# Where the last modulation groups of a three-layer transformer are computed: between output units, or in the waits of three normalisations

## The reference, cut to what matters

```python
def adaln(cond, w, b):                      # w: (1024, 6144)
    m = jax.nn.silu(cond) @ w + b
    return [m[:, None, i * d:(i + 1) * d] for i in range(6)]

def modulate(x, g, shift, scale):
    return rmsnorm(x, g) * (1.0 + scale) + shift

# per layer, for the tokens (and, with its own modulation, for the context)
# sh1, sc1, g1, sh2, sc2, g2 = adaln(cond, ada_w, ada_b)
# x = x + g1 * mixer(modulate(x, norm_mix, sh1, sc1))      mixer: input product, attention, output product
# x = x + g2 * swiglu(modulate(x, norm_ffn, sh2, sc2))     up and gate product, then down product
```

## Time and profile before

| what | value |
|---|---|
| median of three runs | 2565.95 us (2563.1 to 2574.91) |
| the profiled execution, its own time | 2562.09 us |
| its span in the trace | 2560.3 us |
| TensorE busy (matmuls) | 2442.6 us, 95% |
| VectorE, ScalarE, GpSimd busy | 994.0, 850.0, 772.1 us |
| granted TensorE clock, mean | 0.978 |
| DMA | 209.76 MB, mean 82 GB/s |
| modulation weights | 96 loads of 512 KB |

### The profile page before, as it was taken

The page is one execution under the profiler, slowest core; times in us unless marked ns, Lnnn a source line. Parts: engine busy times, 40 slices in busy tenths (PEclk is TensorE's granted clock), DMA queues, the critical chain, the costliest instruction groups (busy, mean ns, idle before and its releaser), DMA issues.

```text
span 2560.3 us, 34062 instructions
## 1 busy us (share of the span) xinstructions
PE 2442.6 (95%) x13345; PEld 1917.4 (75%) x13345; DVE 994.0 (39%) x1426; ACT 850.0 (33%) x1382; POOL 772.1 (30%) x413
## 2 busy tenths in 40 slices
PE   6998999899999999799999989999999998999999
PEld 3676667688888888578666768888887755888887
DVE  4356651411122112435446542121436775523322
ACT  3234652322122122233445432222333464322321
POOL 1151001122222222132011234444453451444443
PEclk9999999899999999899989989999999998999999
DMA  7550006322212213421011123333243300333332
GB/s 260 171 166 26 2 1 214 99 62 62 66 57 66 66 56 124 142 69 52 17 19 31 42 74 96 94 97 99 83 106 83 95 2 17 93 97 99 99 95 78
DMA packets 335970, 209.76 MB, mean 82 GB/s; under 512 B 29299, under 2 KB 308444, under 8 KB 335842
## 3 DMA queue, kind: packets, MB, share of 16 engines
q1 hardware_dynamic: 332880, 201.89, 26.9%
q10 hardware_dynamic: 2898, 6.05, 0.7%
q0 software_dynamic: 64, 0.04, 0.0%
HBM read 205.82 MB, written 2.12 MB: 81 GB/s over the span
## 4 chain that ended last, share of the span: by engine, by line
PE 83%; issue 5%; DVE 5%; DMA 3%; ACT 2%; POOL 2%; SPq 0%; DVEq 0%; ACTq 0%; POOLq 0%
PE G L1544 21%; PE G L1545 21%; PE G L1546 21%; PE G L1731 5%; PE G L1759 4%; PE G L1744 4%; DMA raw<-in_l_ada_w_dram 2%; POOL wlo L873 2%; PE G L1615 1%; PE G L1582 1%; PE G L1702 1%; PE G L1777 1%; DVE ssq L2000 1%; PE G L1566 1%; DVE scr L2099 1%
## 5 line engine op out<-in xcount | busy, mean ns | idle before, releaser
L873 POOL TENSOR_TENSOR wlo<-raw,whi 128x1024 fp32r<-128x1024 f32 x282 | 679.6, 2410 | 1555.6 <-ACT whi L1059 1555.6
L1544 PE MATMUL G<-big_a,whi 128*128 128x512 f32 x2016 | 742.9, 368 | 9.6 <-POOL wlo L873 6.5
L1059 ACT ACTIVATE whi<-raw 128x1024 fp32r<-128x1024 f32 x282 | 298.9, 1060 | 1304.4 <-PE G L1546 1121.1
L1545 PE MATMUL G<-big_a,wlo 128*128 128x512 f32 x2016 | 728.6, 361 | 0.0
L1546 PE MATMUL G<-big_a,whi 128*128 128x512 f32 x2016 | 725.3, 360 | 0.0
L1544 PEld LDWEIGHTS G<-big_a,whi 128*128 128x128 f32 x2016 | 380.4, 189 | 87.9 <-issue 14.9
L1545 PEld LDWEIGHTS G<-big_a,wlo 128*128 128x128 f32 x2016 | 380.3, 189 | 63.6 <-issue 6.7
L1546 PEld LDWEIGHTS G<-big_a,whi 128*128 128x128 f32 x2016 | 379.2, 188 | 60.4
L1544 PE MATMUL G<-big_b,whi 128*128 128x512 f32 x856 | 316.0, 369 | 3.1 <-POOL wlo L873 2.3
L1545 PE MATMUL G<-big_b,wlo 128*128 128x512 f32 x856 | 315.5, 369 | 0.0
L1546 PE MATMUL G<-big_b,whi 128*128 128x512 f32 x856 | 314.3, 367 | 0.0
(11 more groups left out here) (244 smaller groups left out, 2280.1 us busy)
## 6 DMA issues: line engine op xcount, KB each, us to landing
raw<-in_l_ada_w_dram SPq DMA_DIRECT2D x96, 512.0 KB, 5.1
raw<-in_l_ffn_w_gate_dram SPq DMA_DIRECT2D x44, 512.0 KB, 3.8
raw<-in_l_ffn_w_up_dram SPq DMA_DIRECT2D x44, 512.0 KB, 3.8
raw<-in_l_ffn_w_down_dram SPq DMA_DIRECT2D x32, 512.0 KB, 4.0
raw<-in_w_up_dram SPq DMA_DIRECT2D x32, 512.0 KB, 4.0
raw<-in_w_down_dram SPq DMA_DIRECT2D x32, 512.0 KB, 3.7
raw<-in_w_in_dram SPq DMA_DIRECT2D x28, 512.0 KB, 3.8
raw<-in_l_w_in_dram SPq DMA_DIRECT2D x24, 512.0 KB, 3.9
```

The source lines that it names most:

```text
L873: pool.tensor_tensor(wlo[:, u % 2], raw[:, r % RING], whi[:, u % 2].bitcast(F32), ALU.subtract).then_inc(raw_free[r % RING], 1)
L1059: act.activation(whi[:, u % 2], raw[:, r % RING], ACT.Copy).then_inc(hi_done, 1)
L1544: pe.matmul(o, whi[:, u % 2, k], rlo[:, k, t0:t0 + w], start=k == 0, stop=False)
L1545: pe.matmul(o, wlo[:, u % 2, k], rhi[:, k, t0:t0 + w], start=False, stop=False)
```

## The change

Six groups move. (0,10) and (0,11) leave the first input stage, (1,4), (1,5), (1,10) and (1,11) leave the output and down product of layer 0. Each of the second, third and fourth normalisation hosts two of them: (0,10) and (0,11); (1,4) and (1,5); (1,10) and (1,11). The output product of layer 0 still has seven groups, (1,0) to (1,3) and (1,6) to (1,8); the last down product has one, (1,9), after unit 1.

Inside a hosted normalisation the order becomes, on each engine:

- SyncE: weights of first unit, four loads of the early group, weights of second unit, four loads of the late group, weights of third and fourth unit. The ring turns follow this order.
- TensorE: early group, norm matmuls, turn of the early group, spread, late group, first two units, turn of the late group.
- ScalarE: `upper` of the second unit is no longer in the residual loop. Row copy of the early group, root (which now counts `std` itself), `upper` of the second unit, the eight tiles, row copy of the late group.
- VectorE: reciprocal, diagonal, columns of the early group, the eight tiles, columns of the late group.
- GpSimd: same order of subtractions; that of the second unit follows its `upper`.

The spread now shares the PSUM group of the norm matmuls. Which `arow` buffer a group uses follows its place in the new order `ADA_ORDER`. In the feed-forward products of layers 0 and 1 SyncE issues the first four tiles outside its loop. The diff, cut:

```diff
+        def plan_hosted_norm(n):
+            early, late = HOSTED[n]
+            r0 = use_ring()
+            group = plan_aux(("norm", n))
+            plan_ada(*early)
+            plan_aux(("adaT",) + early)
+            r1 = use_ring()
+            plan_aux(("spread", n), group)
+            plan_ada(*late)
+            plan_aux(("adaT",) + late)
+            return r0, r1
...
-        ADA_IN0 = [(0, 4 + i) for i in range(8)]
-        ADA_WOUT0 = [(1, i) for i in range(7)]
-        ADA_DOWN0 = [None] + [(1, 7 + i) for i in range(5)]
+        ADA_IN0 = [(0, 4 + i) for i in range(6)]
+        ADA_WOUT0 = [(1, i) for i in (0, 1, 2, 3, 6, 7, 8)]
+        ADA_DOWN0 = [None, (1, 9)]
+        HOSTED = {1: ((0, 10), (0, 11)), 2: ((1, 4), (1, 5)), 3: ((1, 10), (1, 11))}
+        ADA_ORDER = [(0, i) for i in range(10)] + ADA_WOUT0 + list(HOSTED[1]) + ADA_DOWN0[1:]
+        ADA_ORDER += list(HOSTED[2]) + list(HOSTED[3])
...
         plan_wout(0)
-        plan_norm(1)
-        plan_ffn(0, FFN_CHUNKS, True)
-
-        plan_norm(2)
+        plan_ffn(0, FFN_CHUNKS, True, plan_hosted_norm(1))
+
+        RINGS2 = plan_hosted_norm(2)
...
@@ SyncE
+                    if hosted:
+                        for b in range(4):
+                            m = P * (f0 + b // len(ups))
+                            load(plan["up", l, c, b][1], [(ups[b % len(ups)][:, :, m:m + P], P)])
+                            if b < 2:
+                                ada(*hosted[b])
...
@@ ScalarE
+                if i in HOSTED:
+                    ada(*HOSTED[i][0])
+                    act.wait_ge(*auxiliary(("norm", i)))
+                    act.activation(rsb[:, 1, 0:n // P], ps(("norm", i), n // P), ACT.Sqrt,
+                                   bias=eps[:, 0:1]).then_inc(PH[f"norm{i}", "std"], 1)
+                    upper(plan[second][0])
...
+                if i in HOSTED:
+                    ada(*HOSTED[i][1])
...
-                    upper(plan["wout", l, m][0] + 2)
+                    if l == 2 or m < KD - 1:
+                        upper(plan["wout", l, m][0] + 2)
...
-                        if u < n_split:
+                        if u < n_split and not (l == 0 and last and m == KD - 1):
                             upper(u)
...
@@ TensorE
                 a, g = plan["norm", i]
+                if i in HOSTED:
+                    ada(*HOSTED[i][0])
                 pe.wait_ge(*when((f"res{i}", "ssq"), KD))
...
                 a, g = plan["spread", i]
-                take_group(g)
+                if i in HOSTED:
+                    ada_turn(*HOSTED[i][0])
+                else:
+                    take_group(g)
                 pe.wait_ge(*when((f"norm{i}", "diag"), 1))
...
                 aux(mm)
+                if i in HOSTED:
+                    ada(*HOSTED[i][1])
...
                         first_units([("up", l, 0, 0), ("up", l, 0, 1)], lambda b: ranges, h_ready)
+                        ada_turn(*HOSTED[1 + 2 * l][1])
...
@@ VectorE
+                if i in HOSTED:
+                    ada_columns(*HOSTED[i][0])
                 dve.wait_ge(*auxiliary(("spread", i)))
...
+                if i in HOSTED:
+                    ada_columns(*HOSTED[i][1])
```

More of the change, by code:

```diff
@@ L323, in plan_norm, with plan_inputs @@
             plan_aux(("spread", n))
-        def plan_inputs(st, units, vts, sums, two=(), ada=(), deferred=None):
+        def plan_hosted_norm(n):
[9 more added lines that the diff above has]
+            return r0, r1
+        def plan_inputs(st, units, vts, sums, two=(), ada=(), deferred=None, rings=()):
             seq = []
@@ L331, in plan_inputs @@
                 if n < len(units):
-                    plan_unit((st, "U", n), True, 2 if n in two else 1, early)
+                    plan_unit((st, "U", n), True, 2 if n in two else 1, rings[n] if n < len(rings) else early)
                     early = None
@@ L809, in ffn @@
                 for c, (f0, nf) in enumerate(chunks):
-                    r0 = plan["up", l, c, 0][1]
                     per = 4 // len(ups)
-                    with sp.Fori(0, nf // per) as j:
+                    hosted = HOSTED[1 + 2 * l] if c == 0 and l < 2 else ()
+                    done = 1 if hosted else 0
+                    if hosted:
[4 more added lines that the diff above has]
+                                ada(*hosted[b])
+                    r0 = plan["up", l, c, 4 * done][1]
+                    with sp.Fori(0, nf // per - done) as j:
                         for b in range(4):
                             w = ups[b % len(ups)]
-                            load(r0 + b, [(w[:, :, bass.ds((j * per + (f0 + b // len(ups))) * P, P)], P)], j)
+                            m = f0 + per * done + b // len(ups)
+                            load(r0 + b, [(w[:, :, bass.ds((j * per + m) * P, P)], P)], j)
                     if l == 0 and c == len(chunks) - 1:
@@ L1073, in ada @@
                 act.wait_ge(*product_of(("ada", l, i, 3)))
-                turn = i + 12 * l
+                turn = ADA_ORDER.index((l, i))
                 if turn >= 2:
-                    act.wait_ge(*auxiliary(("adaT", (turn - 2) // 12, (turn - 2) % 12)))
+                    act.wait_ge(*auxiliary(("adaT",) + ADA_ORDER[turn - 2]))
                 key = ("ada", l, i, 3)
@@ L1092, in deferred_root, with norm @@
                                bias=eps[:, 0:1]).then_inc(PH[f"norm{i}", "std"], 1)
-            def norm(i, ranges, shift):
+            def norm(i, ranges, shift, second=None):
                 n = sum(r[1] for r in ranges)
[L1096 to L1100, removed]
+                if i in HOSTED:
[5 more added lines that the diff above has]
+                else:
+                    act.wait_ge(*auxiliary(("norm", i)))
+                    release(act.activation(rsb[:, 1, 0:n // P], ps(("norm", i), n // P), ACT.Sqrt, bias=eps[:, 0:1]),
+                            ("norm", i))
+                    act.wait_ge(gfree[group_of(("norm", i)) % 4], group_of(("norm", i)) // 4 + 1)
+                    act.sem_inc(PH[f"norm{i}", "std"], 1)
                 for k in range(KD):
@@ L1490, in _ @@
             wout(1, 3, TX)
-            norm(3, X_ONLY, lambda k, q: mod[:, 1, 24 + k, q:q + 1])
+            norm(3, X_ONLY, lambda k, q: mod[:, 1, 24 + k, q:q + 1], ("up", 1, 0, 1))
             ffn(1, FFN_CHUNKS, X_ONLY, 4)
@@ L1864, in ffn @@
                         first_units([("up", l, 0, 0), ("up", l, 0, 1)], lambda b: ranges, h_ready)
+                        ada_turn(*HOSTED[1 + 2 * l][1])
                         for b in range(2, 4):
                             unit(("up", l, 0, b), hhi, hlo, ranges)
-                    with pe.Fori(1 if c == 0 else 0, nf // per) as j:
+                    done = 1 if c == 0 else 0
+                    with pe.Fori(0, nf // per - done) as j:
                         for b in range(4):
-                            unit(("up", l, c, b), hhi, hlo, ranges, j=j)
+                            unit(("up", l, c, 4 * done + b), hhi, hlo, ranges, j=j)
                     first = (f"ffn{l}", "lo", tiles)
```

22 lines of the change are left out of this document (13 added, 9 removed).

## The result

The changed kernel takes **2537.54 us** (median of four runs, 2534.86 to 2541.38), where the kernel before takes 2568.28 us (four runs, 2563.1 to 2574.91). The ratio is 0.988, 95% interval 0.9863 to 0.9897. The profiled execution took 2537.89 us, its span 2536.1; that of before 2562.09 and 2560.3. The prediction was 2539, in a range of 2526 to 2554.

What follows compares the result with a forecast made beforehand. TensorE's in-order work and standstills bound the kernel: 21.2 us removed plus 1.8, 1.8 and 0 in the normalisations, 24.8 off 2562.09, gives 2537.3; 1.7 added for timed runs makes 2539, range 2526 to 2554.

Steps and rivals of the forecast that it cites:

- The removed term: Two groups leave the first input stage (5.5 us), four leave layer 0's last down product (15.7 us): 21.2 us saved.
- Nothing takes the groups' place: First input stage: nothing waits behind either removed group's gap, so the full 5.5 us is saved.
- The port term: Each hosted normalisation: moving the second tile's subtraction behind the root frees VectorE's additions of squares, 2.1 us.
- the early group holds the fourth's norm matmuls by 0.6 us: Fourth normalisation: norm matmuls could start at 1491.8, but the early group holds them to 1492.4.
- rival B: Normalisations: subtraction catches the diagonal, or the late group ends later than reckoned; 2 us each, 2545 us; chance 0.12.
- The landing: Fourth load of a hosted group: lands 3.8 us after issue, against at least 3.7 for a load alone.
- rival D: Early and late fourth loads become the wait, six in all; at 12 us landing, 2586 us; chance 0.04.
- Rival C: Groups in the normalisations are not hidden: six pay 3.9 us each, 23.5 us, giving 2562; chance 0.10.
- the second half: Normalisation from the spread on, with the late group: first units 1.8 us earlier in second and third, 0 taken in fourth.
- T + 11.3: Late group's end, counted from the norm matmuls' start T; some 0.3 us after the first tile is ready.
- The bounds there: Fourth normalisation: 1.2 us lost if first units keep their length, 1.5 gained if tiles set their end; 0 taken.
- rival A: Groups in the waits keep TensorE's clock high, speeding spread and first units; about 7 us more, 2532; chance 0.16.

Runs made afterwards that it cites:

- both hosted, old place: Changed kernel, all six groups computed, but the second unit's upper copy stays in the residual loop and its ring turn precedes the early group's: 2554.08 us, ratio 0.9941.

## Why the prediction was right, and where it was not

**The removed term** was 21.2 and is 21.1 by leaving the groups out (15 to 27 by its interval). By the stretches it is 16.2 in the feed-forward part, for 15.7, and in the first input stage 5.8 over three profiles of the changed kernel or 4.7 over nine of kernels that are alike there, for 5.5: 21 to 22. "Nothing takes the groups' place" was not quite so: a wait of 0.61 us has come in behind the last group, in eight of the nine profiles.

**The port term** was 2.1 us in each normalisation and is 2.0, by moving the copy without any group (6.0 in three). With the early group inside, the time from the last unit to the norm matmuls goes from 5.70 to 3.69 in the second. The step that the early group holds the fourth's norm matmuls by 0.6 us was 0.8: 3.49 us with it, 2.72 with none. The Trainium skill ("Trainium Architecture — The Big Picture", What this means for kernel authors) calls the port pair "an exclusive lock (not a bandwidth split)". The trace agrees: the two additions take 4.04 us with a subtraction beside them and 2.02 without. At the new place the diagonal is not held, so rival B's first half is false, but the margin is small. Its second half, a late group that ends later than reckoned, is false too: T + 10.4, 10.2 and 10.5, where 11.3, 11.3 and 10.5 were reckoned. In the second normalisation the subtraction starts 0.16 us after the diagonal's end (469.08, 468.92). In the third, whose two rows from the timeline of the changed kernel follow, it starts 0.27 before it:

```profile
1042.13 0.96 DVE L2056 SCALAR_TENSOR_TENSOR scr<-mats,scr 128x768 f32<-128x768 f32 x1
1042.82 2.46 POOL L898 TENSOR_TENSOR wlo<-raw,whi 128x1024 fp32r<-128x1024 f32 x1 [8.95 <-ACT whi L1084]
```

The diagonal keeps its 0.96 us and the subtraction shows 2.46 instead of 2.34: here the one that runs already goes on, as the prediction had reckoned.

**The landing.** 3.8 was taken for the fourth load. It was 3.86 in the second normalisation and 1463.28 - 1459.46 = 3.82 in the fourth; rival D did not come about. Rival C, groups that are not hidden, fell with the kernels without groups: passages of 93.6 us in sum without any, 93.1 with six.

**Luck in the fourth normalisation.** The first units start at T + 10.46 (1474.72 - 1464.26), predicted T + 10.5, but the parts differ. The norm matmuls take 1.05 us where 1.86 was reckoned, 0.8 less. The upper copy waits 0.46 us for the second tile's weights, a wait that the prediction had at nothing (0.31 us in the second normalisation, row 467.94), and the late group's last load takes 4.1 us for 3.8. The two later profiles show T + 10.87 and T + 10.51.

**What failed is the size of the second half.** The gains of the whole passages were predicted as 1.8, 1.8 and 0 us and measured as 3.8, 3.4 and 1.1; 3.6 in sum against 8.2, and 7.9 over all profiles. The step was "T + 11.3" together with the first units keeping their length:

- The norm matmuls were costed at 2.72 us as before. They take 1.50 behind the early group, because TensorE's clock is up: 1.00 granted in 462.10 to 467.30, where before showed 0.66 in 466.00 to 474.20 and 0.50 in the norm matmuls' own stretch from 471.4 to 474.2. The root, the subtraction and the late group's load all follow from there, so the first units start at T + 10.4 and T + 10.2, not T + 11.3.
- The first units run in a stretch of granted clock 1.00 (0.92 before) and are 1.1 and 0.5 us shorter in the second and third, 2.1 in the fourth (1.00 for 0.83). The prediction had reckoned that tiles which pile up shorten them in the fourth. The clock accounts for it as well: at 0.83, 0.17/0.5 of 13.1 us, 4.5 us, ran at half the rate, which by this estimate costs 2.2 us. The bounds there, 1.2 us lost to 1.5 gained, hold the gain of 1.1.

This is rival A's mechanism, to which I gave 0.16 as a case of its own. Its sign came true: first units at 0.40 us a matmul from the start (0.39 and 0.40 at 476.57 and 476.80). The mechanism came on top of the forecast, and only partly where A put it: the spread, for which A reckoned 1.4 us each, is as slow as before in the second and third normalisation (2.93 us, granted clock 0.59 in the stretch 469.00 to 476.20) and faster in the fourth alone (1.13 for 2.05). The Trainium skill ("TensorE: Matmul & The Clock Gate", What's actually happening) lets recent busyness hold the full clock. The trace agrees for the norm matmuls and the first units, which ran at 1.00 right behind a group; the spread of the second normalisation, behind a gap of 0.75 us, ran at 0.50 (468.97 to 471.80).

**The number itself** came out closer than its parts, by luck. The sum was 4 to 5 us short, 24.8 for 28.7 to 29.8. It was taken from a profiled execution of 2562.09 us that was the fastest of that kernel on record: a second profile has 2569.6 us of span, and the medians of before in the later comparisons are 2567.8 and 2569.6. Adding 1.7 to 2562.09 set the start 4 to 6 us too low (2563.8 for 2567.8 to 2569.6). Two errors of like size and other sign gave 2539 for 2537.5. The timed runs show a gain of 30.7, 28.0 and 27.6 us in the three comparisons.

## What to carry to other kernels

Before work is put into a wait, follow the buffer of its last load: the same six groups gave 28 us with one upper copy behind the root and 14 with it and its ring turn in front. In front it held VectorE's short additions, which alone costs 2 us each time (seen without groups). With groups the early one's last load also had to wait for the copied tile's buffer, and the norm matmuls started 5.9 to 6.6 us later. Look first for what a wait is made of; here moving one copy off the short chain was worth 8.4 us, on top of the 21 us that the six groups had cost at their old places. When a clock-dependent row stands behind work that is added, cost it at both levels instead of the one it had.

## What the runs showed of the hardware that was not expected

- With an early group in the wait of 5 us (16 matmul records with 32 columns of weights) the twelve one-column norm matmuls behind it took 1.50 us at a granted clock of 1.00; without one 2.00 us in the second and 2.72 in the third normalisation. Where the group's last quarter came 5 us after the rest (both hosted, old place) they took 2.72 all the same. Only 1.6 us after the norm matmuls at 1.00, behind a gap of 0.75 us in the second normalisation and none over 0.2 us in the third, the spread took 2.93 us with the stretch at 0.59 and 0.63, while the two matmuls of the fourth's took 1.13 with the stretch at 1.00.
- The last load of an early group landed in 3.8 us, as one alone does. In the fourth normalisation, where the late group's loads and the next tiles' share the queue, the DMA share was 0.85 for 8.1 us at 270 GB/s, and the late group's last three quarters started 1.3 and 2.5 us apart, each after waiting for its load (1469.98, 1471.26, 1473.74).
- One stretch of causal attention, the same instructions in every kernel, took from 155.7 to 162.3 us in the eleven profiles, and the first input stage of nine alike kernels 192.5 to 197.9. A difference of a few us between two profiles has to be read by stretches that the edit touches.
